# A two-layer conditioned decoder step on eight cores: the opening matmuls in four steps, a wait between the first weight tiles and x, and a schedule of its own for the modulation

## The reference

```python
for l in range(DEPTH):                              # DEPTH = 2, D_MODEL = 1024
    mod = silu(c) @ w_ada[l] + b_ada[l]             # (B, 6D): shift, scale, gate, twice
    sh1, sc1, g1, sh2, sc2, g2 = split(mod, 6)
    h = rmsnorm(x, norm_mix[l]) * (1 + sc1) + sh1
    if l % 2 == 0:                                  # mixer 0
        a, xin, bg, cg = split(h @ w_in0)           # 512 columns each
        mix = concat(pool_mixer(a), bg * causal_dwconv(cg * xin)) @ w_out0
    else:                                           # mixer 1: spatial gating
        u, v = split(gelu(h @ w_uv1))
        mix = (u * spatial_gating(rmsnorm(v))) @ w_out1
    x = x + g1 * mix
    h = rmsnorm(x, norm_ffn[l]) * (1 + sc2) + sh2
    ga, va = split(causal_dwconv(h @ ffn_up[l]))    # 5632 columns
    x = x + g2 * ((gelu(ga) * va) @ ffn_down[l])
y = rmsnorm(x, norm_final)
```

## Time and profile before

| | before |
|---|---|
| median of 3 runs | 1558.64 us (1557.53 to 1558.82) |
| profiled execution, its own time | 1556.27 us |
| its span, first to last instruction, slowest core | 1554.6 us (all cores 1548.3 to 1554.6) |
| granted TensorE clock, mean over the span | 0.979 on the slowest core |
| TensorE (PE) busy | 1436.9 us, 92% |
| VectorE (DVE) busy | 1037.4 us, 67% |
| ScalarE (ACT) busy | 793.2 us, 51% |
| GpSimd (POOL) busy | 326.6 us, 21% |

### The profile page before, as it was taken

One profiled execution on the slowest core, in us unless ns is written; L12 is line 12 of the kernel. 1 busy time (PEld: TensorE's weight loads), 2 busy tenths in 40 slices (PEclk: granted clock), 3 DMA queues, 4 the chain that ended last, 5 costly groups with the idle time before them and its releaser, 6 DMA issues.

```text
span 1554.6 us, 26494 instructions; the slowest of 8 cores (1548.3 to 1554.6 us)
## 1 busy us (share of the span) xinstructions
PE 1436.9 (92%) x9294; PEld 752.6 (48%) x9294; DVE 1037.4 (67%) x1071; ACT 793.2 (51%) x966; POOL 326.6 (21%) x769
## 2 busy tenths in 40 slices
PE   1658999999999999999999999999999999999996
PEld 1334544445545544444456566544554444444444
DVE  1656557568687777759754533656768977677886
ACT  2235145457475555737555425445746654664552
POOL 2112112112232122223212101112212222222210
PEclk9979999999999999999999999999999999999998
DMA  9957656654568645445643821644444454446523
GB/s 209 201 133 126 96 83 102 114 95 77 105 111 132 121 69 94 83 82 90 118 71 63 150 42 28 101 79 83 88 80 80 74 87 68 81 76 138 124 45 109
DMA packets 62678, 151.93 MB, mean 98 GB/s; under 512 B 13010, under 2 KB 28498, under 8 KB 62036
## 3 DMA queue, kind: packets, MB, share of 16 engines
q0 software_dynamic: 33984, 120.34, 48.4%
q1 hardware_dynamic: 28564, 29.90, 6.2%
HBM read 252.68 MB, written 17.85 MB: 174 GB/s over the span
## 4 chain that ended last, share of the span: by engine, by line
PE 79%; DVE 6%; ACT 6%; issue 4%; DMA 4%; POOL 1%; DVEq 0%; ACTq 0%; POOLq 0%; SPq 0%
PE pp L382 72%; PE pS L382 5%; PE pN L382 2%; DMA wsl<-w_ada 2%; DMA xb<-xp 1%; ACT hb L401 1%; ACT E L401 1%; ACT Y L401 1%; DVE Y L404 1%; ACT ha L401 1%; DVE Y L408 1%; DVE ha L404 1%; DVE bg L404 1%; DVE xb L408 1%; DVE xb L404 1%
## 5 line engine op out<-in xcount | busy, mean ns | idle before, releaser
L404 DVE SCALAR_TENSOR_TENSOR Y<-E,par_t,Y 128x1184 f32<-128x1184 f32 (+1 forms) x368 | 502.2, 1367 | 246.1 <-ACT Y L401 232.3
L382 PE MATMUL pp<-ha,wsl 128*128 128x512 bf16 (+1 forms) x1840 | 427.6, 384 | 6.8 <-DVE ha L1328 3.8
L382 PE MATMUL pp<-R,wsl 128*128 128x512 bf16 (+2 forms) x1928 | 421.8, 375 | 0.8 <-DVE xb L404 0.4
L382 PE MATMUL pp<-hb,wsl 128*128 128x512 bf16 x1792 | 399.9, 382 | 3.7 <-DVE xb L404 2.9
L401 ACT ACTIVATE E<-pp 128x1024 f32<-128x1024 f32 x192 | 196.1, 1022 | 329.6 <-PE pp L382 325.4
L382 PEld LDWEIGHTS pp<-R,wsl 128*128 128x128 bf16 x1928 | 185.2, 98 | 212.0 <-issue 1.7
L382 PEld LDWEIGHTS pp<-hb,wsl 128*128 128x128 bf16 x1792 | 174.9, 98 | 214.0 <-issue 11.5
L401 ACT ACTIVATE Y<-E,par_t 128x1184 f32<-128x1184 f32 (+1 forms) x184 | 240.6, 1307 | 67.0 <-DVE R L408 17.2
L382 PEld LDWEIGHTS pp<-ha,wsl 128*128 128x128 bf16 x1840 | 176.9, 99 | 201.1 <-issue 21.1
L411 POOL COPY cffn<-E 128x2 f32<-128x2 f32 x176 | 78.2, 444 | 442.5 <-ACT E L401 442.5
L408 DVE TENSOR_TENSOR R<-Y 128x1184 bf16<-128x1184 f32 (+1 forms) x86 | 112.2, 1305 | 5.8 <-ACT Y L401 5.4
(11 more groups left out here) (110 smaller groups left out, 1011.6 us busy)
## 6 DMA issues: line engine op xcount, KB each, us to landing
wsl<-ffn_up POOLq DMA_DIRECT2D x88, 512.0 KB, 5.6
wsl<-w_ada POOLq DMA_DIRECT2D x48, 512.0 KB, 8.2
wsl<-ffn_down POOLq DMA_DIRECT2D x32, 448.0 KB, 4.9
wsl<-w_in POOLq DMA_DIRECT2D x16, 512.0 KB, 8.0
wsl<-w_out POOLq DMA_DIRECT2D x16, 512.0 KB, 6.9
wsl<-ffn_down POOLq DMA_DIRECT2D x16, 512.0 KB, 5.4
wsl<-w_uv POOLq DMA_DIRECT2D x16, 512.0 KB, 6.9
o_ffn_s<-E SPq DMA_DIRECT2D x88, 80.0 KB, 4.9
```

The costliest lines, as they stand in the source:

```text
L382: add("pe", lambda e, l=l, r=r, i=i: e.matmul(out_ap, lhsT=l, rhs=r, start=(start and i == 0), stop=(stop and i == n - 1)), reads=rk, writ ...
L404: add("dve", lambda e: e.scalar_tensor_tensor(out=out, in0=in0, scalar=scalar, in1=in1, op0=op0, op1=op1), reads=reads, writes=writes)
```

## The change

It has five parts.

1. **A key between the first tiles and x.** The DMA of modulation tiles 2 to 5 of layer 0 now *reads* the key `("x", 0, 0, 0)`, which A's x (half 0, block 0) writes.
2. **The opening.** Pieces 0 and 1 stand apart around the first sums; the squares of half 1 are all on ACT (before, every second one was on DVE); `w_in0` tile 0 is asked for before pieces 4 to 7. The affine step that makes `ha` and the opening matmuls go two features at a time: piece 4 + q, then the affines of k = 2q and 2q + 1 for both halves, then (`open_k`) the 8 matmuls of the two features before. `P_open` keeps only what follows them.
3. **The background.** `g_weave` goes. The norm (`gens`) and the pieces (`side`) are counted apart: the norm as before, at most one piece step per pump, against a line that reaches the end at 0.97 of the stage's pumps (in m0A it starts only at 0.4 of them). While `lock` holds, from the sums to the copy of the norm, no new piece starts.
4. **Steps.** The background's squares come two by two rather than four by four, with one more empty step before the sums, one more before `bcast` and one more after `rcopy`. A piece's empty step now stands between its matmuls and its DVE instruction.
5. **m0A** idles 16 steps rather than 10 before B's norm begins.

```diff
@@ _issue
+            rd = []
             if kind == "ada":
                 src = wada_d[spec[1], spec[2]]
+                if spec[1] == 0 and 2 <= spec[2] < 6:
+                    rd = [("x", 0, 0, 0)]
...
-                writes=[("w", s)], dma=True)
+                reads=rd, writes=[("w", s)], dma=True)
@@ pump
-        n, c = BG["subs"][BG["stage"]], BG["calls"][BG["stage"]]
+        (n, m), c = BG["subs"][BG["stage"]], BG["calls"][BG["stage"]]
         target = -(-n * BG["c"] * 20 // max(1, 17 * c))
         while BG["done"] < target:
             if not bg_sub():
                 break
+        f = (BG["c"] / c - BG["s0"]) / (0.97 - BG["s0"])
+        if BG["sdone"] < m * f and not (BG["lock"] and BG["sdone"] % 3 == 0):
+            bg_sub("side", "sdone")
@@ bg_end
         while bg_sub():
             pass
+        while bg_sub("side", "sdone"):
+            pass
@@ g_stats
-            for k0 in (0, 4):
-                sq_main(st, ti, range(k0, k0 + 4))
+            for k0 in range(0, 8, 2):
+                sq_main(st, ti, range(k0, k0 + 2))
                 yield
...
         yield
+        yield
+        BG["lock"] = True
         for ti in range(nt):
             sums(st, ti)
...
         yield
+        yield
         bcast(st)
         yield
         rcopy(st)
         yield
+        yield
+        BG["lock"] = False
@@ g_ada (after its matmuls)
         W.free(slot)
         yield
+        yield
         c = 2 * s
...
         yield
-        yield
@@ new
+    def open_k(st, ks):
+        sl, prs = opn["sl"], opn["prs"]
+        for ti in range(2):
+            for k in ks:
+                for g in range(2):
+                    gemm(PP[prs[g]][:, ti * 512:(ti + 1) * 512], PK(prs[g], ti),
+                         [(wap(sl, k, g), st.h[:, k, ti * 512:(ti + 1) * 512])], [("w", sl)], [hK(st, k, ti)],
+                         start=(k == 0), stop=(k == 7))
@@ program
-        adas(0, 2)
+        adas(0, 1)
         sums(A_, 0)
         rstd_pow(0, 4)
-        adas(2, 3)
+        adas(1, 2)
         bcast_part(0)
         scale_x(0)
-        for k in range(8):
-            if k % 2 == 0:
-                sq_main(A_, 1, (k,))
-            else:
-                stt(A_.h[:, k, 512:1024], xseg(A_, k, 512, 512), 1.0 / 1024, xseg(A_, k, 512, 512), ALU.mult, ALU.mult,
-                    xK(A_, k, 1), hK(A_, k, 1))
-        adas(3, 5)
+        sq_main(A_, 1, range(8))
         sums(A_, 2)
         sums(A_, 1)
         rstd_pow(4, 5)
-        adas(5, 6)
+        adas(2, 3)
         bcast_part(1)
         bcast_part(2)
-        adas(6, 7)
+        scale_x(1)
...
-        scale_x(1)
-        adas(7, 8)
-        for ti in range(2):
-            for k in range(8):
-                affine(ti, k, "act" if k % 2 == 0 else "dve")
+        adas(3, 4)
+        open_get()
+        for q in range(4):
+            adas(4 + q, 5 + q)
+            for ti in range(2):
+                for k in (2 * q, 2 * q + 1):
+                    affine(ti, k, "act" if k % 2 == 0 else "dve")
+            if q >= 1:
+                open_k(A_, (2 * q - 2, 2 * q - 1))
...
-        bg_stage("m0A", [], [g_idle(10), g_weave(norm_gens(B_, 0), ada_gens(0, 8, 18), 1)], True)
+        open_k(A_, (6, 7))
+        bg_stage("m0A", [g_idle(16)] + norm_gens(B_, 0), ada_gens(0, 8, 18), True, 0.4)
...
-        bg_stage("f0A", [], [g_weave(norm_gens(B_, 1), ada_gens(1, 0, 12), 1)], False)
+        bg_stage("f0A", norm_gens(B_, 1), ada_gens(1, 0, 12), False)
```

More of the change, by code:

```diff
@@ L429, in store, with bg_stage, bg_sub @@
         add("sp", lambda e: e.dma_start(out=out, in_=in_), reads=reads, writes=[("out", octr[0])], dma=True)
[L431 to L441, removed]
-            try:
-                next(q[0])
-                if BG["armed"]:
-                    BG["done"] += 1
+    BG = {"gens": [], "side": [], "armed": True, "calls": {}, "subs": {}, "stage": None, "c": 0, "done": 0,
+          "sdone": 0, "lock": False, "s0": 0.0}
+    def bg_stage(name, gens, side, armed, s0=0.0):
+        assert not BG["gens"] and not BG["side"]
+        BG.update(stage=name, gens=list(gens), side=list(side), armed=armed, c=0, done=0, sdone=0, s0=s0)
+    def bg_sub(which="gens", cnt="done"):
+        while BG[which]:
+            try:
+                next(BG[which][0])
+                BG[cnt] += 1
                 return True
             except StopIteration:
-                q.pop(0)
+                BG[which].pop(0)
         return False
@@ L453, in pump @@
         if not BG["armed"]:
-            bg_sub()
             return
@@ L471, in bg_end @@
             pass
-        BG["calls"][BG["stage"]], BG["subs"][BG["stage"]] = BG["c"], BG["done"]
+        while bg_sub("side", "sdone"):
+            pass
+        BG["calls"][BG["stage"]], BG["subs"][BG["stage"]] = BG["c"], (BG["done"], BG["sdone"])
     def run(gen):
@@ L581, in norm_gens @@
         return [g_norm(st, which)]
[L583 to L589, removed]
-                yield
-            except StopIteration:
-                q.pop(0)
     def g_idle(n):
@@ L741, in ext_of, with open_get @@
         return R_t[:, b // 2: b // 2 + 736].bitcast(F32), RK(b, 1472)
+    opn = {}
+    def open_get():
+        opn["sl"] = W.get(("in0", 0))
+        opn["prs"] = [newpair(), newpair()]
+    def open_k(st, ks):
[6 more added lines that the diff above has]
+                         start=(k == 0), stop=(k == 7))
     def mixer0(st):
@@ L758, in P_open @@
         def P_open():
-            sl = slots["a"] = W.get(("in0", 0))
-            prs = [newpair(), newpair()]
-            for ti in range(2):
-                for k in range(8):
[L763 to L766, removed]
+            sl, prs = opn["sl"], opn["prs"]
             for g in range(2):
@@ L1387, in program @@
         hist_load(0, 0)
-        bg_stage("m0B", [], [g_weave(norm_gens(A_, 1), ada_gens(0, 18, 24), 1)], False)
+        bg_stage("m0B", norm_gens(A_, 1), ada_gens(0, 18, 24), False)
         mixer0(B_)
         bg_end()
-        bg_stage("f0A", [], [g_weave(norm_gens(B_, 1), ada_gens(1, 0, 12), 1)], False)
+        bg_stage("f0A", norm_gens(B_, 1), ada_gens(1, 0, 12), False)
         ffn(A_, 0, 8)
@@ L1394, in program @@
         hist_load(1, 0)
-        bg_stage("f0B", [], [g_weave(norm_gens(A_, 0), ada_gens(1, 12, 20), 1)], False)
+        bg_stage("f0B", norm_gens(A_, 0), ada_gens(1, 12, 20), False)
         ffn(B_, 0, 7)
         bg_end()
-        bg_stage("m1A", [], [g_weave(norm_gens(B_, 0), ada_gens(1, 20, 24), 1)], False)
+        bg_stage("m1A", norm_gens(B_, 0), ada_gens(1, 20, 24), False)
         mixer1(A_)
         bg_end()
-        bg_stage("m1B", [], norm_gens(A_, 1), False)
+        bg_stage("m1B", norm_gens(A_, 1), [], False)
         mixer1(B_)
         bg_end()
-        bg_stage("f1A", [], norm_gens(B_, 1), False)
+        bg_stage("f1A", norm_gens(B_, 1), [], False)
         ffn(A_, 1, 8)
         bg_end()
-        bg_stage("f1B", [], [g_final(A_)], False)
+        bg_stage("f1B", [g_final(A_)], [], False)
         ffn(B_, 1, 7, last=True)
```

## The result

The changed kernel takes 1577.93 us, median of 4 runs (1575.45 to 1644.25), against 1558.09 us (1557.45 to 1558.82) for the one before on the same chip: ratio 1.0122, 95% interval 1.0102 to 1.0142. It is 19.8 us slower where 8.7 us faster was forecast, and 1577.9 lies above the range. The profiled execution took 1576.86 us with a span of 1575.3 on core 1, the slowest.

What follows compares the result with a forecast made beforehand. TensorE was taken as the bound, busy 1436.9 of 1554.6 us, with at most 48 to win from 164 to 1250 us. Terms +4.3 (m0A's end), +11.0 (f0A's drain), -24 (waits) give -8.7: 1550 us from 1558.6, range 1536 to 1567.

Steps and rivals of the forecast that it cites:

- T: Opening: time at which x's first half is there, taken as 38 us (between 35.5 and 41) against 17.2 before.
- T + 39: Opening: its end 39 us after T, at 77, 12 us later than before.
- with 1 for the later states: m0A: 1 us allowed for the later pooling states, so the trailing means end at 105 against 108.4.
- its own waits I leave as they are: m0A after the trailing means: its existing waits taken as unchanged; only +3.0 for moved pieces and sums.
- The drains: Pieces left for a stage's end: three whole in m0A costing +4.7 us, four in f0A costing +11.0.
- Rival (c): The drains cost nothing, since PE gets the time back in the next stage: 1536 us, chance 0.13.
- The background's waits, -24: Stages from 164 to 1250 us: half of the 48 us that could be won comes back, -24.
- rival (a): Background: the waits only move, giving 5 us rather than 24; 1569 us, chance 0.17.
- The final stage, "at zero": Last stage: no change expected, its idle time being the end's own chain.
- (b): Whole kernel: gains and drains cancel, a third of the 48 us (16) coming back; 1558 us, chance 0.13.
- (d): Opening: x does go first and the tiles wait for it, opening ends at 55; 1528 us, chance 0.04.
- (e): m0A: B's x comes later than ACT reaches it, costing 0 to 5 us; counted within the range.

Runs made afterwards that it cites:

- e1: Changed kernel with the added key alone taken out; ratio 1.0000 to the kernel before.
- e2: Changed kernel with the load of x's first half issued ahead of the first weight tiles; ratio 0.9984 to the kernel before.
- e7: Changed kernel with the pooling states' loads issued earlier, after piece 3 of the opening instead of after its last; ratio 1.0086 to the kernel before.
- e10: Changed kernel with a piece's empty step back behind its DVE instruction; ratio 1.0059 to the kernel before.
- e13: Changed kernel, key kept, with the edits of e7, e9 and e10 together; ratio 0.9926 to the kernel before.
- e5: Changed kernel with four of f0A's twelve pieces moved to m1A; ratio 1.0080 to the kernel before.
- e14: Kernel before with one edit, the background's squares two by two instead of four by four; ratio 0.9929 to the kernel before.
- e6: Changed kernel with the final norm's old squares by four and old number of empty steps, in f1B alone; ratio 1.0177 to the kernel before.
- e3: Kernel before with the new opening and its key, on the old background; 1579.78 us, ratio 1.0113 to the kernel before.
- e9: Changed kernel without the lock, so pieces may start between a norm's sums and its copy; ratio 1.0017 to the kernel before.

## Why the prediction was wrong, step by step

**T and the opening: right, as a sum.** Issue at 28.9 (forecast "near 28"), use at 41.0 (38, bound 41), end at 78.7 (77), so +13.5 for +12. In the prediction's own terms x came 41.0 - 17.2 = 23.8 us later, not 21, and the rest after x was 47.8 - 37.6 = 10.2 shorter, not 9. Edit by edit the terms are 18.1 for the key (e1) and 65.5 - 60.9 = 4.6 for the new order, because without the key ACT waits for x's second half, and with it it doesn't. That the end fits to 1.7 us is partly luck: T was 3 short, and "T + 39" was to be more, for its own terms give 28.5 + 4 x 2.8 + 0.9 = 40.6, where 37.6 was measured.

x's half took 12.2 us from issue to use, and 9 (12.5 with a tile beside it) had been allowed. The 7.0 us for the half "alone" left out that half 1 and the sample x are issued with it and share the queue: 3.01 MB moved there in that time. The Trainium skill (DMA: Bandwidth & Descriptors, Queues, rings and completion order) has the engines take turns between queues with work. The traces agree as far as they go: x's half needed 15.1 to 15.6 us (before, e1, e2) with 0.68 to 0.74 MB of tiles moving beside it, and 12.2 with 0.29 MB; no run has it without tiles from start to end.

**m0A: the first step that failed.** The sum at its end was to be +4.3 and is +13.5 + 2.4 = +15.9, 11.6 more: 1.5 of the opening and 10.1 of m0A itself. On core 1 the means end at 112.95 instead of 105. What failed is "with 1 for the later states": their loads are issued at 75.8, the one that leads the chain takes 12.14 us to land, ACT stands still for 4.8 + 2.8 + 3.1 us behind them, TensorE for 8.3, and DVE for 4.7 in the means, where no stop over 3 was to be seen. I had the states' lateness against the opening's end in hand, 2 us before it rather than 9, and should have set a whole landing against that lead. e7 shows the size: 7.1 by the medians, and means that end at 105.5. The rest, 10.1 - 7.1 = 3.0, is put down to "its own waits I leave as they are": with the empty step moved, pieces wait for DVE, 10.3 us in six waits, of which 4.4 are the drain that was priced. The cure alone is worth 7.2 (e10), but the cures overlap (e13), so the split into 7.1 and 3.0 is no more than one way to share a common slack.

**The drains: right.** In m0A 3.54 + 0.45 + 0.45 = 4.4 of wait for the 4.7, with three pieces in a row. In f0A 9.13 + 0.45 + 0.45 = 10.0 against 9.4, the clock's share 2.0 (35 matmuls in 9.96 us instead of 35 x 3.62 / 16) against 1.6, and the whole price 11.0 against e5's 12.4 - 1.4 = 11.0. That the last two agree to a tenth is luck, since stage medians vary by more. Rival (c), that they cost nothing, is out.

**The background's waits, -24: the second step that failed.** From m0B to f1A the stages sum to +4.1 + 4.7 - 1.4 - 1.9 - 8.8 + 0.3 = -3.0. Less the drain's 11.0 that is -14.0, so 14 came back, not 24; below 15.3 I had rival (a) decide, and it did. Its mechanism holds only in part: the 14 are real and lie in f0A (-6.3 aside from the drain) and m1B, where TensorE is idle 1.0 of 100 us. m1B's gain is by about half the squares and the steps that they add (e14: 4.9 of 8.8); the rest lies in the other steps, which no run separated. In m0B six pieces and a norm sit in 33 pumps, and there the waits did only change their names: +4.1, of which e10 recovers 3.6. The mistake in the working was one share for all stages. The stages differ by 13 us, and which edit does it was never asked: e14 shows that the two lines on the squares hold a gain of 11 us, and that most of it is in m0A, a stage that I had booked at the means' chain alone. The forecast's own range slipped too: T by 3 and waits by 6 each way is 1541 to 1559, not to 1556.

**The final stage, "at zero": +4.5.** The squares two by two can make it (e14: +5.6 with no other edit), so a price of that edit belonged in the sum. How much of the 4.5 is theirs is open: a wait of 4.19 us for DVE's xb stands at 1478 and is 1.5 at most with the old steps, but these took back only 2.4 (e6), which other kernels show without them, and e3 has 2.0 of the loss with the old final norm.

**The account.** Forecast -8.7, measured +17.4 by stages. The difference of 26.1 is 11.6 in m0A with the opening, 10.0 in the background and 4.5 in the final stage. None of the three failed at a count of steps. The first is a load's landing that was put at 1 us, with waits left as they were; the second is waits that were put at one share for all stages; the third was put at zero, and its cause is open. Rival (a) gave 1569, and 1578 is still 9 above it. (b), (d) and (e) did not happen.

## What to carry to other kernels

A "reads" key added to an earlier instruction is a wait of the later writer: look at who comes first in the program before you call it a head start. When the critical path moves earlier relative to its helpers, price each helper load at its whole time from issue to landing less the lead that is left. And background work that is woven into in-order engines did best here in small portions over all pumps: the lock and the late start left a remainder that ran where nothing hid it, and the moved empty step let each piece wait for DVE.

## What the runs showed of the hardware

- x's half (2.1 MB) took 12.2 us from issue to use in the changed kernel, with 0.29 MB of tiles beside it, and about 15 in all kernels that issue it at the start (used at 17.09, 17.57 and 17.20 us), with 0.68 to 0.74 MB beside it. Holding back all tiles but two changed nothing (e2), since two tiles keep POOL's queue busy for that long.
- Loads issued within a microsecond on SP's queue share it but don't land together: 3.01 MB had moved when the first half of 2.1 MB was used, and in e1 the second half was used 14.2 us after the first.
- The four small loads of the pooling states, issued within 2.2 us of each other beside two halves of B's x, had a landing of 12.14 us in the chain.
- Cures of overlapping waits don't add: 13.1 us together, 22.1 one by one (m0A; e7, e9, e10, e13).
- After TensorE's stop of 9.1 us at f0A's end in the changed kernel the granted clock is 0.50 from 567 to 574 us and 0.90 in the next 4; the 35 matmuls of 128x512 behind it took 9.96 us, 2.0 more than at the 3.62 us per 16 before the stop.
